# Blocks of 33 tiles in place of 32 in a decoder layer's retrieval stage

## The reference, cut to what matters

```python
def _peer(x, w_query, sub_keys, w_down, w_up):
    q = jnp.einsum('td,de->te', xt, w_query).reshape(n_tok, PEER_HEADS, 2, HALF_KEY)
    sc = jnp.einsum('thpk,hpnk->thpn', q, sub_keys).astype(jnp.float32)
    va, ia = lax.top_k(sc[:, :, 0], PEER_TOPK)
    vb, ib = lax.top_k(sc[:, :, 1], PEER_TOPK)
    ...
    top, flat = lax.top_k(cand, PEER_TOPK)
    expert = (jnp.take_along_axis(ia, flat // PEER_TOPK, axis=-1) * N_KEYS
              + jnp.take_along_axis(ib, flat % PEER_TOPK, axis=-1))
    gate = jax.nn.softmax(top, axis=-1).astype(x.dtype)
    ...
        act = _gelu(jnp.einsum('tkd,td->tk', w_down[eb], xb))
        return jnp.einsum('tk,tkd->td', gb * act, w_up[eb])
```

## Time and profile before

| | |
|---|---|
| median of 3 runs | 1553.85 us (1552.78 to 1555.94) |
| the profiled execution's own time | 1548.57 us |
| its span | 1546.8 us |
| TensorE busy | 1523.0 us, 98% |
| VectorE busy | 1161.3 us, 75% |
| ScalarE busy | 639.2 us, 41% |
| GpSimd busy | 755.2 us, 49% |
| DMA | mean 270 GB/s over the span |
| mean granted clock of TensorE | 0.996 |

### The profile page before, as it was taken

The page is one execution under the profiler, slowest core; times in us unless marked ns, Lnnn a source line. Parts: engine busy times, 40 slices in busy tenths (PEclk is TensorE's granted clock), DMA queues, the critical chain, the costliest instruction groups (busy, mean ns, idle before and its releaser), DMA issues.

```text
span 1546.8 us, 23591 instructions
## 1 busy us (share of the span) xinstructions
PE 1523.0 (98%) x8620; PEld 1370.9 (89%) x8620; DVE 1161.3 (75%) x2400; ACT 639.2 (41%) x852; POOL 755.2 (49%) x469
## 2 busy tenths in 40 slices
PE   9999999999999999999999999999999999999996
PEld 8888899889899999999999999988888888888885
DVE  5564262477999978796877866888888888888786
ACT  5323244422234457436643663443333333333333
POOL 2543471324345887868787777632222322222230
PEclk9999999999999999999999999999999999999998
DMA  8532250333246988999899889999999999999981
GB/s 314 185 109 82 95 177 24 113 124 109 82 136 199 336 301 301 351 416 355 304 374 415 326 305 377 321 360 345 348 352 341 353 340 341 351 346 352 376 323 55
DMA packets 145821, 418.24 MB, mean 270 GB/s; under 512 B 17952, under 2 KB 52016, under 8 KB 145200
## 3 DMA queue, kind: packets, MB, share of 16 engines
q1 hardware_dynamic: 100216, 252.84, 46.7%
q0 software_dynamic: 39168, 142.62, 24.9%
q10 hardware_dynamic: 6328, 21.33, 3.5%
HBM read 371.36 MB, written 45.37 MB: 269 GB/s over the span
## 4 chain that ended last, share of the span: by engine, by line
PE 74%; DVE 12%; DMA 8%; POOL 3%; issue 2%; ACT 1%; DVEq 0%; SPq 0%; ACTq 0%
PE ps L1751 11%; PE ps L1750 11%; PE ps L1749 11%; PE ps L433 6%; PE ps L435 6%; PE ps L434 6%; PE ps L1318 5%; PE ps L1319 5%; PE ps L1320 5%; DMA raw<-in_down_t 4%; DMA rows<-in_w_down,expert 2%; POOL w_lo L1542 2%; DMA act_d<-act_t 2%; PE ps L1702 1%; PE ps L1704 1%
## 5 line engine op out<-in xcount | busy, mean ns | idle before, releaser
L1581 ACT ACTIVATE w_hi<-raw 128x1024 fp32r<-128x1024 f32 x252 | 266.6, 1058 | 358.8 <-PE ps L1751 303.1
L1318 PE MATMUL ps<-b_hi,w_hi 128*128 128x368 f32 x1024 | 341.6, 334 | 2.4 <-ACT act_t L1587 2.3
L1319 PE MATMUL ps<-b_lo,w_hi 128*128 128x368 f32 x1024 | 337.2, 329 | 0.0
L1320 PE MATMUL ps<-b_hi,w_lo 128*128 128x368 f32 x1024 | 337.0, 329 | 0.0
L1542 POOL TENSOR_TENSOR w_lo<-raw,w_hi 128x1024 fp32r<-128x1024 f32 x119 | 286.9, 2412 | 77.8 <-ACT w_hi L1581 76.0
L1555 POOL DMA_INDIRECT rows<-in_w_up,expert x128 | 150.1, 1173 | 341.0 <-DVE ps L1870 330.8
L1751 PE MATMUL ps<-w_hi,b_lo 128*128 128x512 f32 x768 | 298.8, 389 | 0.0
L1750 PE MATMUL ps<-w_lo,b_hi 128*128 128x512 f32 x768 | 298.8, 389 | 0.0
L1749 PE MATMUL ps<-w_hi,b_hi 128*128 128x512 f32 x768 | 298.8, 389 | 0.0
L1791 DVE SCALAR_TENSOR_TENSOR rows<-rows,ps 128x1024 f32<-128x1024 f32 x144 | 174.9, 1218 | 101.2 <-DMA rows<-in_w_down,expert 76.5
L1877 DVE TENSOR_TENSOR w_lo<-raw,w_hi 128x1024 fp32r<-128x1024 f32 x133 | 162.8, 1224 | 70.2 <-ACT w_hi L1581 70.1
(11 more groups left out here) (288 smaller groups left out, 2512.1 us busy)
## 6 DMA issues: line engine op xcount, KB each, us to landing
raw<-in_down_t SPq DMA_DIRECT2D x128, 512.0 KB
raw<-in_up_t SPq DMA_DIRECT2D x128, 512.0 KB
raw<-in_units SPq DMA_DIRECT2D x75, 512.0 KB, 3.3
act_d<-act_t SPq DMA_DIRECT2D x124, 192.0 KB
c<-act_d SPq DMA_DIRECT2D x124, 192.0 KB
gate_d<-gmat ACTq DMA_DIRECT2D x32, 512.0 KB
v<-gate_d SPq DMA_DIRECT2D x16, 512.0 KB
i<-gate_d SPq DMA_DIRECT2D x16, 512.0 KB
```

The costliest lines, as they stand in the source:

```text
L1318: nc.tensor.matmul(out, ring.w_hi[:, s, w], b_hi[:, c, 0:T], start=c == 0, stop=False)
L1319: nc.tensor.matmul(out, ring.w_hi[:, s, w], b_lo[:, c, 0:T], start=False, stop=False)
L1320: last = nc.tensor.matmul(out, ring.w_lo[:, s, w], b_hi[:, c, 0:T], start=False, stop=c == KC - 1)
L1581: nc.scalar.activation(w_hi[:, u % W4, :], raw[:, u % W4, :], ACT.Copy).then_inc(hi_done, 1)
```

## The change

Five groups of numbers change; no instruction is added or taken away. A block has 33 tiles, 17 of them ahead of the rounds. The turn of the picks stands ahead of tile 15 of a block, the three tiles of the extra tokens' path `ASK_TILE` and `DOT_TILE` by three and `COEF_TILE` by two tiles later, as are, by two, the extra rounds and the products. `BLOCK_DOTS` has 41 entries for 40. The exponent's tile and `SPLIT_TILE` stay.

```diff
-BLOCK_TILES = 32
-CHOICE_TILES = 16
+BLOCK_TILES = 33
+CHOICE_TILES = 17
 EXP_TILE = 6
-TURN_TILE = 14
+TURN_TILE = 15
 SPLIT_TILE = 120
...
-ASK_TILE, DOT_TILE, COEF_TILE = 90, 107, 113
-X_ROUND_TILES = (116, 119)
-PRODUCT_TILE = 121
+ASK_TILE, DOT_TILE, COEF_TILE = 93, 110, 115
+X_ROUND_TILES = (118, 121)
+PRODUCT_TILE = 123
...
-BLOCK_DOTS = tuple(range(1, 17)) + (16,) + tuple(i for i in range(17, 32) for _ in range(1 + (i % 2 == 0 or i == 31)))
+BLOCK_DOTS = tuple(range(1, 18)) + (17,) + tuple(i for i in range(18, 33) for _ in range(1 + (i % 2 or i == 32)))
```

## The result

The changed kernel took **1542.61 us** (median of 4 runs, 1540.33 to 1543.78), the kernel before beside it 1553.67 (1552.78 to 1555.94). The direction was right, the size was not. Among the later runs three executions (1892 and 6743 us of the kernel with its tail alone, 1893 us of the kernel before beside it) fell in a slower state, and no ratio or median in this text has them.

A forecast was written before the change was run, and what follows sets the result against it. TensorE was taken to set the pace. Gains of 4.0 (turn) and 1.6 (rounds), less 1.9 in the tail, made 3.7 us: 1553.85 - 3.7 = 1550.2 us, range 1545.5 to 1555.5.

The forecast's parts named there:

- The turn: Picks of block 0, taken one tile later: 2.2 us of waiting and 1.8 of slow clock go, gain 4.0 us.
- The low part of tile 27: GpSimd's low part of the weights near 547: hidden by 1.2 us; a wait for it would be a sign against.
- The rounds: Blocks 1 and 2, rounds starting at tile 17: waits at L1702 go, gain 1.6 us, bounds 0 and 1.6.
- L1318: Waits of 2.3 us in the crowded stretch: gain taken as 0, bounds 0 and 2.3.
- The tail: Extra rounds behind the last block: waits and slow clock grow from 2.1 to 4.0 us, a loss of 1.9.
- The issue: SyncE's issue of the x_coef load in the tail: at 950.7, bound 952.9.
- the burst: GpSimd's four gathers in one tile, ahead of the tail: same as before, its wait 1.0 us in place of 3.16.
- VectorE 9.8 us: First extra round: from x_coef landing to operands ready, signal included, 9.8 us as before; ready at 967.9.
- the first rival: Tail keeps TensorE's pace: operands in time, gain 7.7 us, end 1546.2; chance 0.20.
- The difference of 5.3 us taken over: Whole kernel: median before lies 5.3 us above the profiled execution; assumed the same after the change.
- Slower (0.10): Rival in the tail: x_coef queues behind raw weights, 9.7 us more, end 6.0 late at 1559.9; chance 0.10.
- The estimate of 2.0 us: Load of the coefficients by the skill's rule: 2.0 us against the row's 7.3, giving 1546.2; the forecast kept the row.

The follow-up runs named there:

- the kernel with its tail alone: Kernel before, turn and blocks of 32 kept, with COEF_TILE 115, extra rounds behind tiles 118 and 121, products at 123: 1550.35 us, ratio 0.9989.
- the second profile: Kernel before, unchanged, profiled again and timed beside itself: 1552.58 us, ratio 0.9993; the profiled execution took 1555.31.
- the kernel without the plain tile: Changed kernel with the rounds of a block starting at its tile 16 again (CHOICE_TILES 16), all else as changed: 1549.28 us, ratio 0.9981.
- the one with the turn alone: Kernel before with TURN_TILE 15 in place of 14 and nothing else: 1555.38 us, ratio 1.0013.
- all together, with the split: Changed kernel with SPLIT_TILE 117 and each row asked one tile sooner in the part with rounds: 1536.75 us, ratio 0.9895.

## Why the prediction was wrong

**The turn: right against the profile that was read, lucky in its size.** Forecast a gain of 4.0 us. Gelu 24 to gelu 27 took 16.19 us before and 12.31 after, 3.9 less. The turn came 1.8 us behind the picks, as forecast. The low part of tile 27 made no one wait, and the clock was full. But the prediction took the 4.0 us for a fixed cost, since VectorE gets to the picks "by its own work and the gathers". Of the cast 2.7 us are GpSimd's stretch. The turn's cost is 2.4 us in the second profile, where the clock stayed full, and nothing in that of the tail alone, where the cast took 0.23 us.

**The rounds: right in these waits, short in what lies behind them.** The 1.6 us at L1702 are gone, as taken. The expected cause, ScalarE's copy, is shown by the kernel without the plain tile, where its line is back at 1.7. That kernel also has 4.7 us for VectorE's operands, with the plain tile behind its rounds and not ahead of them. I had said that the first round meets VectorE at the absolute time at which it did, and read no further. By the kernel's own lists a row is not asked for sooner in blocks of 33: from its asking to its use there are 1.67 tiles in the mean in both kernels. What is new is a tile's time, 4.0 us, in each block ahead of the rounds, in which VectorE and the gathers go on while TensorE needs nothing of them. The kernel with `SPLIT_TILE = 117` and the turn moved shows what this is for: TensorE comes some 2 us earlier to rounds that hang on rows, and at one of them it is handed back.

**L1318: 0 taken, 0.8 measured** (2.3 to 1.5), inside the bounds.

**The tail: this step failed.** "TensorE waits 2.4 us where it waited 1.5", 1.6 for the clock: 4.0 in sum. It waited 0. The issue (950.4 for 950.7) and the landing (7.0 for 7.3) hold; so does the burst, whose wait of 3.16 is 0.51 where 1.0 was taken. What was mis-sized is "VectorE 9.8 us", taken over from before as if it were work. Of it 5.4 was the stretch of the products, 7.28 in place of 1.89. After, only one of the three products meets the start of a low part (961.97) where two did before, and the set takes 5.14: 2.1 us less. With 0.3 each from issue and landing, and a tenth for the signal, that is 2.9 to 3.0, against a forecast wait of 2.4. The margin is 0.3 us (964.9 to 965.2), so the first round is in time by little, and some luck is in it: with the turn put back it waited 0.9. That the 7.28 is no work is shown in the same kernel too, where the same set took 4.60 in the second profile. At the second round, GpSimd's low parts end with tile 119, and the round stands two tiles later: the products take 2.14 us. The kernel before with `SPLIT_TILE = 117` shows that freeing this set alone removes the second wait; it gained 3.9 us by the ratio, 1.4 to 6.5 by its interval. This is the first rival, to which I had given 0.20, for its own reason, "what GpSimd does at that moment decides".

**The difference of 5.3 us taken over: this step failed too.** It stood between the profiled execution of before and the median. The prediction took it for something that the change does not touch; after the change it is 2.3. The profiled execution of before was one of its fastest, and its tail was another one than usual: waits of 1.5 and 0.6 with a full clock. The second profile, at 1555.31, has a wait of 3.7 and 3.4 us lost by low clock; so has the one with the turn alone. The tail costs 5.0 us more in it, just where the change acts. So the first rival's 1546.2 is too high as well. That the kernel before varies by its low clock shows in its other executions too, of which 103 were timed in the runs above: 20 with a mean granted clock of 0.997 have a median of 1549.6 us, 25 with 0.993 or 0.994 one of 1555.2. The changed kernel, at 0.996 to 0.998 in all ten of its executions, has 1539.7 to 1544.2.

From the second profile the sum is: turn 6.68 - 4.31 = 2.4 (the clock stayed full there), tail 7.1, L1702 2.5, L1318 1.0 less 1.5, together 11.5, and the stages differ by 576.01 - 564.28 = 11.7; the medians differ by 11.1. This pair agrees best with them, but it is one of four: two profiles of each kernel give stages shorter by 7.7 (573.34 and 565.7) to 11.7 us.

By these two steps: against the profiled execution 1544.9 was forecast and 1540.33 measured, 4.6 less, of which 4.0 is the tail and 0.8 L1318. The other 3.0 of the 7.6 is what the offset of the median shrank by, 5.3 before and 2.3 after. How much of these 3.0 is a low clock that the change took away, and how much is that each profile is one execution, no run divides.

**Slower (0.10):** `x_coef` did not queue; it took 7.0 us. The estimate of 2.0 us that the prediction set against its row did not hold either. The Trainium skill, page "DMA: Bandwidth & Descriptors", section "Anatomy of one DMA", gives that sum for transfers that GpSimd issues, and this one is SyncE's.

**Still open.** The edits overlap: rows asked sooner alone win 10 to 11 us, by the tail and the rounds; blocks of 33 win 11, by these and the turn; all together, with the split, 16. How much of the change's share comes from VectorE's extra tile of time ahead of the rounds, and how much from fewer collisions with GpSimd, no run here divides. The turn's 2.3 us in the changed kernel are shown by the traces, not by the times, whose intervals (0.9957 and 0.9942) overlap. Why the turn alone gained nothing is shown at one round, in one profile of a kernel with the split beside it, and by the two profiles in which the picks were early anyway; how often they are, and the rest of it, stays open.

## What to carry to other kernels

Before a wait is taken over from one profile into a sum, take a second profile of the same kernel: a short chain that ends close to its deadline can cost 2 us in one execution and 7 in the next, and a wait of 2.2 us can be absent from a third. A duration of an instruction that another engine stretches is not work; look at what stood beside it and price it alone. And a tile won at one place is kept only if everything that meets TensorE behind it is early by as much: here the turn moved alone paid nothing, and one line that asks for gathered rows a tile sooner was worth as much as the whole change.

## What the runs showed of the hardware

A VectorE product of 1024 bf16 elements with both inputs in SBUF takes 0.6 to 0.7 us alone. One that meets the start of a GpSimd low part of 2.4 us takes up to 3.5 us and ends some 0.6 us after it. The first product of the kernel before ran from 957.30 to 960.79, with a low part from 957.80 to 960.23. It had begun 0.5 us before the low part, and was held all the same; the low parts themselves took 2.35 to 2.62 us with or without a product beside them. The cast of the picks, from f32 to f16 in SBUF, takes 0.23 us alone and 2.91 beside one. The rows of VectorE with one input in PSUM (L1791) take 1.22 us in either case.

The clock fell behind waits of TensorE, not always behind the same length. Behind 3.6 to 5.2 us it fell each time, for some 6.8 us (0.57 over 8 us). Behind 1.9 us at L1717 it fell for 3.4. Behind the wait at the turn, 2.1 to 2.2 us, it fell in two profiles (0.66 over 5 us) and stayed at 1.00 in three others; it stayed there too behind two waits of 2.0 us at L1702.
